# A mixture-of-experts block on one core: the gather reads the residual, ten slots of weights ahead

## The reference

```
x = x + merged @ w_o
t = rmsnorm(x, g_ffn)
logits = t @ w_router + b_router
top_v, top_i = top_k(logits, 4);  combine = softmax(top_v) put at top_i       # 256 x 32
for e in range(32):
    gu = t @ w_gate_up[e] + b_gate_up[e]                # 256 x 2048
    gate, up = min(gu[:, :1024], 7), clip(gu[:, 1024:], -7, 7)
    y = ((up + 1) * gate * sigmoid(1.702 * gate)) @ w_down[e] + b_down[e]
    out += combine[:, e] * y
return rmsnorm(x + out, g_final)
```

## Time and profile before

| | |
|---|---|
| median of 3 runs | 1260.73 us (1258.7 to 1262.66) |
| the profiled execution | 1260.54 us, span 1258.7 us |
| PE busy | 1160.9 us (92%) |
| DVE, ACT, POOL busy | 344.6, 246.0 and 138.5 us |
| DMA | 450.22 MB, mean 358 GB/s |
| chain that ended last | PE 57%, DMA 35% |

### The profile page before, as it was taken

The page is one execution under the profiler, slowest core; times in us unless marked ns, Lnnn a source line. Parts: engine busy times, 40 slices in busy tenths (PEclk is TensorE's granted clock), DMA queues, the critical chain, the costliest instruction groups (busy, mean ns, idle before and its releaser), DMA issues.

```text
span 1258.7 us, 14525 instructions
## 1 busy us (share of the span) xinstructions
PE 1160.9 (92%) x6394; PEld 603.1 (48%) x6394; DVE 344.6 (27%) x546; ACT 246.0 (20%) x362; POOL 138.5 (11%) x78
## 2 busy tenths in 40 slices
PE   4989999999899999999999999989999999899985
PEld 4988999998433333343333333333333333333321
DVE  5885988563301101021010101011110101010101
ACT  4436566534101000001000000001000000000002
POOL 5343333564000000000000000000000000000000
PEclk9989899999899999999999999999999999999998
DMA  9844444558799999999999999999999999999993
GB/s 252 276 135 135 134 135 135 188 182 326 310 409 428 427 427 428 427 428 426 429 427 428 426 428 428 427 428 427 429 425 429 426 427 429 427 428 427 429 425 148
DMA packets 74081, 450.22 MB, mean 358 GB/s; under 512 B 7344, under 2 KB 48384, under 8 KB 49440
## 3 DMA queue, kind: packets, MB, share of 16 engines
q1 hardware_dynamic: 73296, 447.03, 86.9%
q0 software_dynamic: 720, 2.23, 0.6%
HBM read 448.19 MB, written 1.05 MB: 357 GB/s over the span
## 4 chain that ended last, share of the span: by engine, by line
PE 57%; DMA 35%; ACT 2%; DVE 2%; POOL 2%; issue 1%; SPq 0%; DVEq 0%; ACTq 0%
DMA slot<-in_w_gate_up 35%; PE pj L1171 16%; PE pj L1024 15%; PE gb L1194 12%; PE gb L1159 3%; PE pt L1201 2%; PE s L1201 2%; PE pj L1183 1%; PE ga L1159 1%; ACT w_hi L455 1%; POOL w_lo L388 1%; DMA mix<-in_w_in 1%; PE s L1066 1%; PE pj L1166 1%; DVE w_lo L665 1%
## 5 line engine op out<-in xcount | busy, mean ns | idle before, releaser
L1171 PE MATMUL pj<-slot,GL 128*64 128x512 f32 x2048 | 456.1, 596 | 49.7 <-DMA slot<-in_w_gate_up 49.7
L1171 PEld LDWEIGHTS pj<-slot,GL 128*64 128x64 f32 x2048 | 139.7, 137 | 349.7 <-issue 252.8
L912 DVE TENSOR_SCALAR V<-pj 128x512 f32<-128x512 f32 x32 | 22.1, 692 | 775.4 <-PE pj L1171 775.4
L1194 PE MATMUL gb<-slot,V 128*64 128x512 f32 x1024 | 227.0, 596 | 0.7 <-ACT V L573 0.7
L1194 PEld LDWEIGHTS gb<-slot,V 128*64 128x64 f32 x1024 | 70.7, 137 | 153.2 <-issue 129.6
L1024 PE MATMUL pj<-hT_hi,w_hi 128*128 128x256 f32 x448 | 130.9, 292 | 13.2 <-DVE hT_lo L670 7.4
L388 POOL TENSOR_TENSOR w_lo<-mix,w_hi 128x1024 fp32r<-128x1024 f32 x40 | 115.3, 2884 | 167.4 <-ACT w_hi L455 167.4
L1024 PE MATMUL pj<-hT_lo,w_hi 128*128 128x256 f32 x448 | 128.4, 287 | 0.0
L1024 PE MATMUL pj<-hT_hi,w_lo 128*128 128x256 f32 x448 | 128.3, 286 | 0.0
L569 ACT ACTIVATE V<-V 128x512 f32<-128x512 f32 x32 | 20.2, 630 | 520.6 <-DVE V L912 514.3
L419 POOL DMA_DIRECT2D slot<-in_g_final x1 | 0.6, 593 | 885.1 <-PE pj L1171 885.1
(11 more groups left out here) (280 smaller groups left out, 1015.1 us busy)
## 6 DMA issues: line engine op xcount, KB each, us to landing
slot<-in_w_gate_up SPq DMA_DIRECT2D x128, 2048.0 KB, 41.7
slot<-in_w_down SPq DMA_DIRECT2D x64, 2048.0 KB, 43.4
mix<-in_w_in SPq DMA_DIRECT2D x28, 1024.0 KB, 6.2
mix<-in_w_lru_out SPq DMA_DIRECT2D x4, 1024.0 KB, 5.0
mix<-in_w_fox_out SPq DMA_DIRECT2D x4, 1024.0 KB, 5.6
mix<-in_w_o SPq DMA_DIRECT2D x4, 1024.0 KB, 5.2
x_sb<-in_x SPq DMA_DIRECT2D x2, 512.0 KB, 4.2
out<-x_sb SPq DMA_DIRECT2D x2, 512.0 KB, 2.6
```

Of the source, the lines that this page charges most:

```text
L912: v.tensor_scalar(gate, pj[0][:, :], LIMIT, None, ALU.min).then_inc(gate_ready, 1)
L1171: last = mm(pj[q // 2][h:h + SLOTS, :], hg[:, c, i, :], w[:, q * 512:(q + 1) * 512], start=False, stop=(c == GU_CHUNKS - 1))
L1194: last = mm(gb[h:h + SLOTS, :], actT[:, f % 4, f // 4, :], w[:, a * D + q * 512:a * D + (q + 1) * 512], start=(f == 0), stop=(f == KT - 1))
```

## The change

- The residual after the projection goes to a tile of its own, `x2`, and not back to `x_sb`. Within each block of 256 columns it holds the even columns first, then the odd ones, which is the order in which the 2 MB pieces hold the rows of w_gate_up. w_router and g_ffn are brought to the same order.
- The gather reads `x2`. `sel` holds the reciprocal RMS in place of 1, and g_ffn is applied when `ga` and `gb` are copied to `hg`: four ACT operations with a scale, one DVE product. `h2` and its scaling are gone. Gate-up waits for the second half only at its fifth chunk.
- b_down is added within each expert's `down` by a one-hot product, as the gate-up bias is. It is loaded by four more DMAs of POOL and split in two fp32r parts by ACT and POOL.
- `open_sums` is gone. The first scatter opens the banks, and the residual is added by `add_residual` at experts 20 to 23.
- `slot9` is free behind the last residual add, so ten pieces are loaded ahead, and the slots follow in plain order. Its last user is now piece 189, the last one of gate-up. The last piece is loaded in two halves.
- Two groups of the routing products run within the output projection. DVE makes the last copy to `h2T`. Three small activations load the tables for Sqrt, Exp and Sigmoid early. Positions count from 1, and the scaling of the top value stands behind the mask.

```
-SLOT_OF = [*range(FIRST_SLOTS)] + [CYCLE[q % N_SLOTS] for q in range(ALL_PIECES - FIRST_SLOTS)]
+SLOT_OF = [q % N_SLOTS for q in range(ALL_PIECES)]
...
-            free_after[lg_at] = lambda: sp.wait_ge(sums_open, 1)
+            free_after[lg_at] = lambda: (sp.wait_ge(ylru_ready, 1), sp.wait_ge(dve_evac, C_WO - C_WL + 4))
...
+            def load_last_piece(e, m, s):
+                sp.dma_start(slot[s][:, 0:CHUNK], piece_src(e, m)[:, 0:CHUNK]).then_inc(loaded[s], 16)
+                sp.dma_start(slot[s][:, CHUNK:], piece_src(e, m)[:, CHUNK:]).then_inc(end_loaded, 16)
...
-            g.wait_ge(ylru_ready, 1)
-            g.dma_start(gffn_b, g_ffn.rearrange("(a n) -> a n", a=1).broadcast_to([P, D])).then_inc(late_loaded, 16)
-            g.dma_start(bdn, b_down[:, :]).then_inc(late_loaded, 16)
...
+            for i in range(4):
+                g.dma_start(bdn_raw[i * N_EXP:(i + 1) * N_EXP, :], b_down[:, i // 2 * 512:(i // 2 + 1) * 512]).then_inc(late_loaded, 16)
...
+            g.wait_ge(bgu_part_ready, 2)
+            g.tensor_tensor(bdn[:, :], bdn_raw, bdn_part[:, :].bitcast(F32), ALU.subtract).then_inc(bdn_split, 1)
-            g.wait_ge(h2_scaled, 1)
-            g.tensor_tensor(h2_rows(0), h2_rows(0), by_row(gffn_b), ALU.mult).then_inc(h2_ready[0], 1)
-            g.wait_ge(chunk_done, MIX_CHUNKS + 2 * LAST_USER[LG_SLOT] + 2)
+            g.wait_ge(chunk_done, MIX_CHUNKS + 2 * LAST_USER[END_SLOT] + 2)
...
             def hg_copy(p):
                 act.wait_ge(gathered, p * 2 + 1)
-                act.activation(hg[:, 0:KT // 2, :, :], ga[:, :].rearrange("p (k i s) -> p k i s", i=2, s=SLOTS),
-                               ACT.Identity).then_inc(hga_ready, 1)
+                for k in range(KT // 2):
+                    ins = act.activation(hg[:, k, :, :], ga[:, k * P:(k + 1) * P].rearrange("p (i s) -> p i s", i=2), ACT.Identity,
+                                         scale=gain[:, k // 2, k % 2:k % 2 + 1])
+                ins.then_inc(hga_ready, 1)
...
-            v.tensor_scalar(stat[:, 30:32], top8[:, :, TOP_K], -1.0, None, ALU.mult).then_inc(neg_top, 1)
             for t in range(TT):
                 link(v.match_replace(rep[:, t, :], top8[:, t, :], lg[:, t, :], -BIG))
             v.tensor_tensor(msk, rep[:, :, TOP_K:], lg[:, :, TOP_K:], ALU.not_equal).then_inc(mask_ready, 1)
+            v.tensor_scalar(stat[:, 30:32], top8[:, :, TOP_K], -1.0, None, ALU.mult).then_inc(neg_top, 1)
...
             def build_sel(p):
+                for t in range(TT):
+                    for i in range(2):
+                        e = 2 * p + i
+                        ins = v.tensor_scalar(sel[:, t, i, :], iota[:, 0, :], pos[:, t, e:e + 1], stat[:, 26 + t:27 + t], ALU.is_equal,
+                                              ALU.mult)
+                ins.then_inc(sel_ready, 1)
...
                 if n % 2 and p < PAIRS:
+                    hg_copy(p)
+                    if p + 1 < PAIRS:
+                        build_sel(p + 1)
+                    dve.wait_ge(selw_transposed, p)
+                    weigh_sel(p)
+                    dve.wait_ge(chunk_done, n * EXP_CHUNKS + (MIX_CHUNKS + GU_CHUNKS + 1))
                     build_onehot(p)
...
+                if c > 1:
+                    pe.wait_ge(h2T_ready, c - 1)
+                    for t in range(TT):
+                        route(c - 2, t)
...
-            def open_sums():
-                pe.wait_ge(combT_ready, 1)
-                pe.wait_ge(flag_ready, 1)
-                for t in range(TT):
-                    for h in range(2):
-                        mm(acc[t][h][:, :], combT[:, t * P:(t + 1) * P], bdn[:, h * 512:(h + 1) * 512], start=True, stop=True,
-                           skip_group_check=True)
-                        last = mm(acc[t][h][:, :], ident[:, :], x_sb[:, t, h * 512:(h + 1) * 512], start=False, stop=True,
-                                  skip_group_check=True)
-                last.then_inc(sums_open, 1)
+            def add_residual(t, h):
+                for m in range(2):
+                    c0 = h * 512 + m * CC
+                    mm(acc[t][h][:, m * CC:(m + 1) * CC], ident[:, :], x2[:, t, c0:c0 + CC].rearrange("q (i n) -> q n i", i=2),
+                       start=False, stop=True, skip_group_check=True)
...
             def gate_up(i, chunk_at, pair=None):
...
+                    if c == KT // 2 and pair is not None:
+                        pe.wait_ge(hgb_ready, pair + 1)
...
+            def down(i, chunk_at):
+                mm(gb[:, :], onehot[:, i, :], bdn[:, :], start=True, stop=False)
...
+                if 20 <= n < 20 + 2 * TT:
+                    add_residual((n - 20) // 2, n % 2)
```

More of the change, by code:

```diff
@@ L169, in hybrid_block @@
         slot = [alias(f"slot{i}", [P, 2 * CHUNK], F32, at) for i, at in enumerate(slot_at)]
-        LG_SLOT = FIRST_SLOTS
-        yo = x_sb
-        def by_row(t):
-            return t.rearrange("q (n i) -> q i n", i=2)
-        def h2_rows(t):
-            return h2[:, t, :].rearrange("q (i n) -> q i n", i=2)
+        END_SLOT = N_SLOTS - 1
+        yo = slot[END_SLOT][:, 2048:4096].rearrange("p (t d) -> p t d", t=TT)
         h2T = Q
-        bgu_raw = alias("bgu_raw", [P, 1024], F32, probs_at)[:, :]
+        raw = alias("raw", [P, 1536], F32, probs_at)
+        bgu_raw, bdn_raw = raw[:, 0:1024], raw[:, 1024:1536]
         bgu = alias("bgu", [P, 1024], F32R, probs_at)
+        bdn = alias("bdn", [P, 512], F32R, probs_at + 4 * 1024)
         bgu_part = alias("bgu_part", [P, 1024], F32R, v_at + 4 * 1024)
-        gffn_b = flat(LG)[:, 0:1024]
-        bdn = flat(LG)[0:N_EXP, 1024:2048]
-        gfin_b = slot[LG_SLOT][:, 0:D]
-        junk = slot[LG_SLOT][:, D:D + 512]
+        bdn_part = alias("bdn_part", [P, 512], F32R, gl_at + 4 * 512)
+        gfin_b = slot[END_SLOT][:, 0:D]
+        junk = slot[END_SLOT][:, D:D + 512]
         gate = flat(V)[:, 0:512]
@@ L207, in hybrid_block @@
         ones = flat(V)[:, 640:768]
[L208 to L210 removed]
+        comb = flat(GL)[:, 1920:1920 + TT * N_EXP].rearrange("p (t e) -> p t e", t=TT)
+        pos = flat(GL)[:, 1792:1792 + TT * N_EXP].rearrange("p (t e) -> p t e", t=TT)
+        sq = [flat(GL)[:, 0:CC], flat(GL)[:, CC:2 * CC]]
+        g4 = alias("g4", [4, 2 * P], F32, lg_at)
+        gain = vec[:, V_GFFN:V_GFFN + KT].rearrange("p (i m) -> p m i", i=2)
+        nothing = stat[:, 68:69]
         pj = [bank("pj0"), bank("pj1")]
@@ L834, in _ @@
             split_lower(C_WO + 1)
+            link(v.memset(lg[:, :, 0:TOP_K], BIG))
             for c in range(4):
@@ new lines, in build_sel, with weigh_sel, build_sel_at @@
+                ins.then_inc(sel_ready, 1)
+            def weigh_sel(p):
+                for t in range(TT):
+                    for i in range(2):
+                        e = 2 * p + i
+                        ins = v.tensor_scalar(selW[:, t, i, :].rearrange("p (u s) -> p u s", u=2), iota[:, :, :], pos[:, t, e:e + 1],
+                                              comb[:, t, e:e + 1], ALU.is_equal, ALU.mult)
+                ins.then_inc(selw_ready, 1)
+            def build_sel_at(p, marks):
@@ new lines, in build_sel_at, with weigh_sel_at @@
+                dve.wait_ge(marked, marks + 1)
+                v.tensor_tensor(sel.rearrange("p t i s -> p t (i s)"), sel.rearrange("p t i s -> p t (i s)"),
+                                stat[:, 26:28].unsqueeze(2).broadcast_to([P, TT, P]), ALU.mult).then_inc(sel_ready, 1)
+            def weigh_sel_at(p, marks):
+                wide = [P, 2, 2, SLOTS]
+                halves = [selW[:, t, :, :].rearrange("p i (u s) -> p i u s", u=2) for t in range(TT)]
+                for t in range(TT):
+                    v.tensor_tensor(halves[t], iota[:, :, :].unsqueeze(1).broadcast_to(wide),
+                                    pos[:, t, bass.ds(p * 2, 2)].unsqueeze(2).unsqueeze(3).broadcast_to(wide),
+                                    ALU.is_equal).then_inc(marked, 1)
+                dve.wait_ge(marked, marks + 3)
+                for t in range(TT):
+                    ins = v.tensor_tensor(halves[t], halves[t],
+                                          comb[:, t, bass.ds(p * 2, 2)].unsqueeze(2).unsqueeze(3).broadcast_to(wide), ALU.mult)
@@ L987, in _ @@
             pe.wait_ge(rows_loaded, 112)
-            nc.tensor.transpose(ga[:, 0:NVEC], rows[:, :], ident[0:NVEC, 0:NVEC]).then_inc(vec_psum, 1)
+            for i in range(2):
+                nc.tensor.transpose(ga[:, NVEC + 4 * i:NVEC + 4 * i + 4], g4[:, :].rearrange("m (n i) -> m i n", i=2)[:, i, :], ident[0:4, 0:4])
+            nc.tensor.transpose(ga[:, 0:NVEC], rows[0:NVEC, :], ident[0:NVEC, 0:NVEC]).then_inc(vec_psum, 1)
             for j in range(KT):
@@ L1201, in scatter @@
                     last = mm(acc[t][q][:, :], selWT[h:h + SLOTS, i, t * P:(t + 1) * P], Y[h:h + SLOTS, :],
-                              start=False, stop=True, skip_group_check=True)
```

(4 more changed lines are left out.)

196 lines of the change are left out of this document (93 added, 103 removed).

## The result

The changed kernel takes 1251.39 us (median of 5 runs, 1249.07 to 1253.22); the kernel before, with the runs made beside it, 1260.72 (5 runs, 1258.02 to 1262.66). The ratio is 0.993, 95% interval 0.9911 to 0.9949: 9.3 us faster, where 8.7 were predicted (1252.0). The interval leaves out 1, so the gain is clear of the noise. The profiled execution took 1249.07 us, with a span of 1247.0.

The account below looks back on a forecast made before the run. The stream of 192 pieces at 428 GB/s was taken as the bound. From 1260.54: -9.5 holes, +1.7 POOL's loads, -1.2 g_final, +0.35 tail make 1251.9, given as 1252.0; range 1248.5 to 1256.0.

Parts of the forecast that it names:

- The bound, and the holes: The piece stream sets the end; of 10.5 us lost in holes at 324-336 and 358-362 us, 9.5 close.
- g_final: Its 0.52 MB load near the end moves behind the last gate-up piece, out of the full stream: -1.2 us.
- Expert 0's start: Shorter chain from 304 to 328 us: expert 0 begins at 325.0 on the old clock, 2.9 us earlier.
- the terms up to sel: Chain ahead of expert 0: routing ends at 314.75, mask at 316.6, sel at 319.2 against 321.2 us today.
- sel's four operations: In build_sel, four 128x64 operations replace one 128x256 of 0.43 us; taken as 0.7 us.
- the gather: Both halves ahead of expert 0, the first at half clock, kept at 5.7 us; bounds 3.9 and 7.6.
- The 1.78 us stall: Scale of the top value, ahead of the mask: POOL's L417 leaves and the scale moves behind the mask, gain 1.8 us.
- GpSimd's four loads: POOL's four new bdn_raw issues stand ahead of chunk 34's split: net +1.7 us for stream and chain, bounds 1.0 and 2.4.
- The second hole: At 358-362 us, 1.7 us lost; closes as open_sums leaves expert 0, piece 14 being issued by 348.2.
- The strided x2 writes: DVE's residual add of 0.70 us ahead of the routing: put at nothing, +0.7 at most.
- The tail: After the last gate-up piece, the one-hot product in the last down adds 0.35 us.
- Case 4: PE, with 2.2 us an expert to spare, becomes the second half's bound through new waits: 1268 us, chance 0.04.

Follow-up runs that it names:

- e1: Changed kernel with the slot order of before, so nine pieces ahead and g_final's load back in the full stream; 1258.73 us, ratio 0.9983.
- e9: Changed kernel with products that nothing reads added on TensorE at the routing, to keep its clock up; 1250.84 us, ratio 0.9912.
- e2: Kernel before with one edit, the scaling of the top value moved behind the mask; 1261.57 us, ratio 1.0004.
- e5: Changed kernel with all eight bias loads issued by SyncE instead of GpSimd; 1252.32 us, ratio 0.9926.
- e6: Changed kernel with g_final loaded into a buffer of its own after expert 19, inside the full stream; 1253.79 us, ratio 0.9943.
- e4: Changed kernel with the one-hot product for b_down made nine times in each expert; 1270.16 us, a single run.
- e3: Changed kernel with the one-hot product for b_down made five times in each expert; 1252.57 us, ratio 0.9937.
- e12: Changed kernel with the edits of e5, e9, e10 and e11 together; 1253.27 us, ratio 0.9935.
- e13: Changed kernel with the edits of e5, e9 and e11 together, without e10's; 1251.39 us, ratio 0.9915.
- e10: Changed kernel with the weight splits of mixer chunks 6 and 7 moved ahead in VectorE's list; 1255.19 us, ratio 0.9948.
- e11: Changed kernel with 27 identity products on TensorE ahead of chunk 0; 1250.8 us, ratio 0.992.

## Why the prediction was right, point by point

- **The bound, and the holes: right.** Time went with the stream. Closed: 9.6 us against 9.5, and e1, without the tenth slot and with g_final's load back in the stream, is slower than the changed kernel by 7.3 (by the ratios 6.7). The pace of the second half is unchanged.
- **Expert 0's start: 2.2 us earlier, not 2.9.** From the end of the last mixer chunk to expert 0 it is 14.95 us (310.11 to 325.06) against 17.83 (310.06 to 327.89), which looks like the 2.9. But the prediction had put one group of the routing, 0.9, ahead of the last chunk, and this stretch leaves it out. From the start of chunk 37 (290.93, before 291.56) it is 34.1 us against 36.3. Counted from there, the terms up to sel hold: routing ended after 22.8 us (predicted 314.75 - 291.56 = 23.2), mask after 24.8 (25.0), sel after 27.8 (27.6). For sel's four operations I had 0.7 and it took 0.98. Here the skill's page was nearer: the Trainium skill, "VectorE: DVE Perf Modes", section on the TRN2 errata, gave an estimated 0.90 for the four. What failed is the gather, 6.3 us and not 5.7: its first half is 3.78 as before, its second 2.55 in place of 1.92, since TensorE's granted clock is still 0.50 up to 324 us and 1.00 only then. With the clock up the two take 3.8 (e9).
- **The routing ahead of the last chunk holds up the stream too: a term that I had left out.** I counted it on expert 0's chain alone. But the eighth and ninth piece are issued when the last chunk is done (310.05 before, 310.11 after), and by then the 0.63 us by which chunk 37 was early are gone: 0.7 us. By landings, the ninth piece comes 61.9 us after SyncE's first issue of an expert's piece in the kernel before and 63.1 after it in the changed one; the 1.2 are these 0.7 and the 0.5 of the loads.
- **The 1.78 us stall: the gain was right, the cause I had open.** It was GpSimd's product (e2). The prediction listed two reasons, the scale's new place and L417's leaving; only the second counts.
- **GpSimd's four loads: mis-sized.** Predicted +1.7. The issues take 1.98 us, but the affine select behind them no longer falls beside a VectorE operation (0.29 in place of 1.36), and the split takes 2.39 in place of 2.82. Chunk 34 begins at 271.15 against 271.78, while the trace of after was 1.1 us ahead already at 226 us (225.93 against 227.04): a net cost of 0.5. I had the split's part and overlooked the select's. By e5 the cost of all eight is 1.25.
- **The second hole: right.** None is seen, and down begins with its one-hot product at 343.91, where I had 344.0. No run puts open_sums back alone, so that it made the second hole is read from the trace and not tested.
- **The strided x2 writes: put at nothing, and hidden.** VectorE's add takes 1.07 us at 310.11 where it took 0.70. It ends at 311.18, and PE, busy with the routing, wants the columns at 311.32.
- **g_final: about right.** -1.2; e6 gives 1.5 to 1.7 by its times, 1.4 by landings, as the price of the load inside the stream. Nothing waits for it at the end: from ACT's table load to VectorE's last steps it is 4.8 us in both (1235.69 to 1240.47, and 1247.40 to 1252.19).
- **The tail: the wrong sign in the profile.** Predicted +0.35; from the landing to the end it is 27.98 us against 29.06. The new product is there, 0.43. But in the tail before, the last expert's transposes and open scatter ran at a lower clock (granted 0.90 from the landing to the table load, 1.00 after): the transposes took 1.13 where they take 0.75. It is no chance of one run: the three profiled kernels with the old order of slots (before, e1, e2) have 0.90 or 0.91 there and a tail of 29.1 to 29.5 us, those with the new order, e4 aside, 1.00 and 27.9 to 28.9. Why the order of slots should move the clock is not shown.
- **Case 4, PE as the bound: its cover was mis-sized.** It gave 2.2 us an expert; e3 and e4 show 1.3 over the run. The change stayed clear of it, since the work that it adds to each expert is 0.43 long. But the point from which the case decides was nearer than I said. Slower than before by 3.8 us takes 0.4 an expert beyond the cover: 1.7 of further work, not 2.6; e4, with 1.85, is slower than before by 9.8 on the same chip, in its one run.
- **The profiled run.** It is 11.5 us shorter than the one before, where 8.6 were predicted and the medians show 9.3. By stages: 1.1 ahead of all edits, 0.5 back for the loads, 0.7 back for the routing ahead of the last chunk, 9.6 for the holes, 1.2 for g_final, 1.1 in the tail, and 0.2 back outside the span. These make 11.6. So the mechanism was right, and that the medians came within 0.6 of the forecast is in part luck: the loads cost 1.2 less than I had put and the tail 1.4 less, and the routing cost 0.7 that my sum didn't have. Put right by these, the sum would have been a gain of 10.5, further from the medians' 9.3.

## What to carry to other kernels

When a stream of loads sets the end, count the microseconds in which it runs below its rate and ask of each edit which of them it closes: here one more buffer, filled before the stall, closed 5 us of hole and with the place of g_final's load was worth 7, and all the rest of the change 1.6. Check a small dip in the mean rate by the times at which the pieces land: one of 0.9 us delayed no piece, and the runs that closed it (e9, e12, e13) got nothing for it that shows. Count an engine's cover over the whole run and its lead, not per step. Before you move an operation that takes ten times its usual time, look at what another engine does at that moment: the stall belongs to the meeting, and can be handed to the next operation in line.

## What the runs showed that I had not expected

- **VectorE and GpSimd stand still for each other.** The held operation waits until GpSimd's has ended and then does its own work. It ends 0.02 us after GpSimd's for the scale of 0.16 (before), 0.09 for the mask of 0.22 (e2), 0.15 and 0.28 for operations of 0.29 and 0.42 (e10), and 1.08 for the split of 1.22 (at 64.03, after). GpSimd waits in the same way when VectorE is first: its split takes 3.44 us at 261.55 in the kernel before, behind a VectorE split at 261.51, and 2.40 where it meets none. The Trainium skill, "SBUF — State Buffer", section "Who interferes with whom", says that the two share one pair of ports as an exclusive lock, and that VectorE contends when it has two inputs in SBUF (the mask) or runs in a mode of two ports. The traces agree: the loser waits to the end, it is not slowed in proportion. Operations with one input are held too, the 128x2 scale, L741 in e10 and the cast at 77.28; that they ran in such a mode is what the rule would need, and no run here shows it.
- **The start of a run moves its time.** Over the profiled runs the first weights, on their way from 4.19 us on, take 8.33 (after), 8.56 (before), 8.81 (e13), 9.39 (e11), 9.98 (e10) and 10.34 us (e9) to land, and all that follows is later by as much. Chunks behind an idle stretch add to it: the two behind the idle times before 20 and 67 us, where the granted clock is 0.50 to 0.65, took 7.55 and 7.46 in after and 8.32 and 8.15 in e9; 5.75 is one at full clock. For e9 the two parts make 2.0 + 1.5 = 3.5 us, and SyncE's first issue of an expert's piece does come 3.4 later than in after (267.40 against 263.97). The clock's part is less sure than the landing's: in the kernel before chunk 0 takes 7.95 though the trace grants 1.00 there, and in e11 7.3 at full clock. The two together come near the spread of some 4 us among runs of one kernel, and more than most of the single edits above.
- **One expert in seven or eight takes longer, in every kernel.** In the stretch that the stream bounds, one expert takes 29.4 us by SyncE's groups, and about one in eight 30.4 (after, twice) or 30.8 (e13, twice, seven experts apart). By landings it goes on through the whole stream, four times in each of the two, and costs some 1.5 us each time. A part of the spread of a last landing may be whether one more falls ahead of it. The cause stays open.
